# Inverse root of the variance for ten tiles: Newton's steps on GpSimd, where ScalarE took the root and VectorE the reciprocal

## What is computed

```python
def layer_norm(x, g, b):
    mu = jnp.mean(xf, axis=-1, keepdims=True)
    var = jnp.mean(jnp.square(xf - mu), axis=-1, keepdims=True)
    return (xf - mu) * lax.rsqrt(var + LN_EPS) * g + b
...
# in trunk_layer: 16 experts, each token goes to two of them
x = layer_norm(ALPHA * x + m, ln1_g, ln1_b)
x = layer_norm(ALPHA * x + hier_moe(x, w_router_group, w_router_expert, moe_w1, moe_w3, moe_w2),
               ln2_g, ln2_b)
```

## Time and profile before

| what | us |
|---|---|
| median of 3 runs | 1248.2 |
| lowest and highest of them | 1243.39, 1250.84 |
| the profiled execution | 1245.41 |
| its span, first to last instruction | 1243.7 |
| TensorE busy in the span | 1138.6 |
| VectorE busy | 788.6 |
| ScalarE busy | 536.3 |
| GpSimd busy | 183.1 |

### The profile page before, as it was taken

How to read it: one execution, slowest core, us unless ns; L and a number is a source line. 1 busy time by engine, 2 the same in 40 slices (tenths; PEclk the granted TensorE clock), 3 DMA queues, 4 the chain that set the end, 5 groups by cost and what they waited for, 6 DMA issues and landing times. The chain is left out here.

```text
span 1243.7 us, 20594 instructions
## 1 busy us (share of the span) xinstructions
PE 1138.6 (92%) x5700; PEld 1015.2 (82%) x5701; DVE 788.6 (63%) x1510; ACT 536.3 (43%) x686; POOL 183.1 (15%) x189
## 2 busy tenths in 40 slices
PE   6999999999999999999999974989998999899980
PEld 6999999999999999788888763768886777677760
DVE  4666454564465366566666467666754888778875
ACT  4464344444345346122222223445544756656530
POOL 1000000000000001003322224015001131222222
PEclk9999999999999999999999986899999999999995
DMA  5332598676946635425443316574766789877654
GB/s 182 123 102 65 129 159 117 75 155 85 118 87 223 243 100 180 144 83 175 151 137 135 89 69 243 201 290 171 264 249 251 273 277 339 299 286 272 218 204 152
DMA packets 86987, 221.06 MB, mean 178 GB/s; under 512 B 18992, under 2 KB 45648, under 8 KB 80656
## 3 DMA queue, kind: packets, MB, share of 16 engines
q1 hardware_dynamic: 57824, 129.90, 31.1%
q0 software_dynamic: 18160, 59.53, 14.3%
q10 hardware_dynamic: 10944, 30.95, 12.9%
HBM read 133.75 MB, written 86.58 MB: 177 GB/s over the span
## 5 line engine op out<-in xcount | busy, mean ns | idle before, releaser
L1391 PE MATMUL ps_h<-w_hi,xt_hi 128*128 (+1 forms) x328 | 135.2, 412 | 9.7 <-DVE w_lo L1048 6.2
L1391 PE MATMUL ps_h<-w_lo,xt_hi 128*128 (+1 forms) x328 | 131.0, 399 | 0.0
L1391 PE MATMUL ps_h<-w_hi,xt_lo 128*128 (+1 forms) x328 | 130.9, 399 | 0.0
L286 PE MATMUL ps_vb_c<-x_hi,w_hi 128*128 (+1 forms) x320 | 114.5, 358 | 10.9 <-DVE x_lo L460 10.9
L286 PE MATMUL ps_vb_c<-x_hi,w_lo 128*128 (+1 forms) x320 | 113.6, 355 | 0.0
L286 PE MATMUL ps_vb_c<-x_lo,w_hi 128*128 (+1 forms) x320 | 112.9, 353 | 0.0
L286 PE MATMUL ps_va_b<-x_hi,w_lo 128*128 (+1 forms) x320 | 112.7, 352 | 0.0
L286 PE MATMUL ps_va_b<-x_hi,w_hi 128*128 (+1 forms) x320 | 112.6, 352 | 0.0
L286 PE MATMUL ps_va_b<-x_lo,w_hi 128*128 (+1 forms) x320 | 111.8, 349 | 0.0
L1391 PEld LDWEIGHTS ps_h<-w_hi,xt_hi 128*128 128x128 f32 x328 | 63.5, 194 | 26.4 <-issue 13.9
L1048 DVE TENSOR_TENSOR w_lo<-w_raw,w_hi 128x2048 f32 (+1 forms) x32 | 73.1, 2287 | 6.8 <-ACT w_hi L1043 5.1
(11 more groups left out here) (337 smaller groups left out, 2622.4 us busy)
## 6 DMA issues: line engine op xcount, KB each, us to landing
w_raw<-in_w SPq DMA_DIRECT2D x48, 1024.0 KB
o_scr<-x_raw ACTq DMA_DIRECT2D x42, 512.0 KB, 8.0
w_lo_p<-xs_scr SPq DMA_DIRECT2D x41, 512.0 KB
o_scr<-w_lo_p SPq DMA_DIRECT2D x41, 512.0 KB
w_raw<-in_w_in POOLq DMA_DIRECT2D x19, 512.0 KB, 3.6
xs_scr<-x_raw ACTq DMA_DIRECT2D x17, 512.0 KB, 9.9
x_raw<-in_x_t SPq DMA_DIRECT2D x20, 416.0 KB, 3.4
x_hi_p<-y_scr SPq DMA_DIRECT2D x16, 512.0 KB, 4.3
```

The source lines that it names most:

```text
L286: mm = pe.matmul(ps[i][:, 0:CHUNK], w[:, i, k], x[:, k, bass.ds(c * CHUNK, CHUNK)], start=(k == 0 and n == 0), stop=(k == KT - 1 and n == 2))
L1391: mm = pe.matmul(ps_h[par][:], x[:, par, k], w[:, bass.ds(at, 1), k].rearrange("p o n -> p (o n)"), start=(k == 0 and n == 0), stop=(k == ...
```

## The change

For tiles 0 to 9 the root and the reciprocal are replaced. A new function `inverse_root` on GpSimd computes 1/sqrt(variance + constant) itself: it adds the constant, halves the bits of the number as an integer and subtracts them from a magic constant, which gives a first guess, and refines it by three of Newton's steps of two instructions each. With a last multiplication for the sign and the factors gathered on the way it is ten instructions on a column of 128 rows by one element. Each counts up the semaphore `s_nwt`, and the next waits for it. The chain waits for the aggregate (`s_mv`) and its last instruction counts up `s_rstd`, for which VectorE's second half of the normalisation waits, as before.

The chain is called in GpSimd's step ahead of `fetch` and `put`. ScalarE's `root` and its idle Silu, and VectorE's reciprocal, remain for tiles 10 to 16 (`known`).

```diff
+        def known(tile):
+
+            return isinstance(tile[0], int) and tile[0] >= FPAIR
...
+            def inverse_root(tile):
...
+                pool.wait_ge(s_mv, 1)
+                pool.wait_ge(s_mv, there)
+                at = [done]
+
+                def then(ins):
+                    ins.then_inc(s_nwt, 1)
+                    at[0] = count(pool, at[0] + 1)
+                    pool.wait_ge(s_nwt, 1)
+                    pool.wait_ge(s_nwt, at[0])
+
+                then(pool.tensor_scalar(t, mv[0:n, m, 1:2], LN_EPS, None, ALU.add))
+                then(pool.tensor_copy(bits, t.bitcast(I32)))
+                then(pool.tensor_scalar(guess, bits, -0.5, float(0x5f3759df), ALU.mult, ALU.add))
+                last = guess.bitcast(F32)
+                for i, (to, three) in enumerate(((y, 3.0), (nwt[0:n, 3:4], 12.0), (nwt[0:n, 4:5], 768.0))):
+                    then(pool.tensor_scalar(a, last, last, t, ALU.mult, ALU.mult))
+                    then(pool.tensor_scalar(to, a, -three, last, ALU.add, ALU.mult))
+                    last = to
+                pool.tensor_scalar(rstd[0:n, m:m + 1], last, -1.0 / 8192, None, ALU.mult).then_inc(s_rstd, 1)
...
                     stored = (h, h - 1) if par == 0 else (h, h)
+                    if add and not known(add):
+                        inverse_root(add)
 
                     if get:
                         fetch(get, stored)
...
-                if tiles and tiles[1]:
+                if tiles and tiles[1] and known(tiles[1]):
                     root(tiles[1])
...
-                dve.wait_ge(s_std, f + 1)
-                dve.reciprocal(rstd[0:n, m:m + 1], std[0:n, m:m + 1]).then_inc(s_rstd, 1)
+                if known(tile):
+                    dve.wait_ge(s_std, f + (1 - FPAIR))
+                    dve.reciprocal(rstd[0:n, m:m + 1], std[0:n, m:m + 1]).then_inc(s_rstd, 1)
```

More of the change, by code:

```diff
@@ L1114, in moe_phase @@
         std, rstd = sb("std2", [P, 2]), sb("rstd2", [P, 2])
+        nwt, nwt_i = sb("nwt", [P, 6]), sb("nwt_i", [P, 1], I32)
         eps, idle = sb("eps2", [P, 1]), sb("idle", [P, 1])
@@ L1133, in moe_phase @@
         s_v = [sem(f"s_v{i}") for i in range(5)]
+        s_nwt = sem("s_nwt")
         s_sum, s_bn, s_mv, s_std, s_rstd, s_fx, s_fn, s_y = (
@@ L1310, in fetch @@
                     pool.indirect_dma_start(to, None, o_scr[0:STEPS * P], bass.IndirectOffsetOnAxis(at, 0)).then_inc(s_v[b], 16)
+            def inverse_root(tile):
+                f, m = tile[0], tile[2] % 2
+                n = TAIL if early(f, 1) else P
+                t, y, a = nwt[0:n, 0:1], nwt[0:n, 1:2], nwt[0:n, 2:3]
+                bits, guess = nwt[0:n, 5:6], nwt_i[0:n]
+                done = count(pool, f * 9)
+                there = count(pool, f + 1)
+                pool.wait_ge(s_mv, 1)
[15 more added lines that the diff above has]
+                pool.tensor_scalar(rstd[0:n, m:m + 1], last, -1.0 / 8192, None, ALU.mult).then_inc(s_rstd, 1)
             def put(tile):
```

## The result

The change makes the kernel slower: median 1288.1 us of 4 runs against 1247.0 us of 4 of the kernel before on the same chip, **ratio 1.035 [1.032, 1.038]**, 41 us. The prediction was 1265 with a range from 1246 to 1290: right side, right place, and less than half the size. The profiled execution took 1286.20 us (span 1284.5, mean granted clock 0.945, was 0.962), 40.8 more than that of before.

A forecast was written before the change was run, and what follows sets the result against it. TensorE and VectorE together were taken to bound the stretch. Split intervals 12.9, plus 7.0 before tile 10, minus 1 of gain, made +18.9 us on 1245.4, or 1264.3; 1265 was forecast, range 1246 to 1290.

The forecast's parts named there:

- The queue: In GpSimd's queue the chain stands ahead of the next tile's COPY and two gathers, so the next row sum waits.
- The chain: GpSimd's ten dependent instructions: 0.4 us each, 10.4 us in a step with a weight split, 4.1 without.
- Tiles 5, 6 and 8: Tiles without a split: loop of 17.3 to 18.8 us against intervals of 21.6 and 22.1, adding nothing.
- Before tile 10: Tile 10's sum, one step after tile 9's, starts 7.4 us late, 7.0 after 0.4 to spare; landing 6.5.
- the subtraction of 12.0 us: VectorE idles 2.9 us per pair; 2.0 counted as made good in each of six split intervals, taken off the loss.
- the loop (25.2): From sum to sum with a split: statistics 2.84, chain 10.4, fetch 3.9, landing 8.0 us, against an interval of 21.2.
- the landing: Time from the second gather's end to the next row sum in pairs with a split, taken as 8.0 us.
- rival B: The cover holds: landing 5.3 us, instruction 0.28, loop 21.3; only tile 9 is late; 1245 to 1253 us, 22%.
- the fetch: GpSimd's COPY of row numbers to the end of the second gather, behind the chain, taken as 3.9 us.
- C: ScalarE's relief sends splits and weight transfers out earlier; a third of 30 us comes through: 1238 us, 5%.
- D: From about 0.55 us per instruction the chain itself is late and VectorE waits on it directly: 1278 to 1295, 13%.
- A: The forecast itself: the gathers come late, 1255 to 1285 us, 60%.

The follow-up runs named there:

- wait_only: The kernel before, with GpSimd waiting for the tile's aggregate ahead of the fetch for tiles 0 to 9, computing nothing; ratio 1.003.
- chain_after_fetch: The changed kernel with GpSimd's chain moved behind the fetch; ratio 1.006 to the kernel before.
- half_weights: The changed kernel with half the bytes in each transfer of the next weights from the third expert on; ratio 1.023 to the kernel before.
- split_5_5: The changed kernel with the chain cut in two, five instructions ahead of the fetch and five behind it; ratio 1.008 to the kernel before.
- one_step: The changed kernel with one of Newton's steps instead of three, six chain instructions instead of ten; ratio 1.019 to the kernel before.
- four_more: The changed kernel with four copies of the guess's instruction added, 14 in the chain; ratio 1.040 to the kernel before.
- root_kept: The changed kernel with root and reciprocal kept for all tiles and the chain writing an unused column; ratio 1.035 to the kernel before.
- no_root: The kernel before without root, table loads and idle Silu for tiles 0 to 9, reciprocal of a constant, no chain; ratio 0.996.

## Why the prediction was right in place and wrong in size

**What held.** The queue was the mechanism: the fetch behind the chain, shown by wait_only against chain_after_fetch. The chain has 0.34 to 0.53 us from start to start (predicted 0.4), 10.0 us with a split, once 11.6 (10.4), and 4.4 without (4.1). It is held by L1048, L1048 and L1057 as drawn. Tiles 5, 6 and 8 add nothing. Before tile 10 VectorE waits 5.2 us and the interval grows by 5.3 (7.0 predicted, a landing of 4.4 us where 6.5 was taken). GpSimd's timeline of the changed kernel, tile 10's second gather:

```profile
1204.01 0.98 POOL L1316 DMA_INDIRECT x_raw<-o_scr,id_f  x1 [0.30 <-issue]
```

And VectorE's timeline, tile 10's sum:

```profile
1209.36 1.23 DVE L1611 TENSOR_TENSOR w_hi_p<-w_hi_p,x_raw 128x1024 f32<-128x1024 f32 x1 [5.19 <-DMA x_raw<-o_scr,id_f]
```

**The step that failed first is the subtraction of 12.0 us, "what VectorE can make good".** The sum had set the loop (25.2) against the interval (21.2). When a loop is the longer of the two it is the interval, and VectorE's gaps already lie inside the landing, beside which it waits. The idle time shows it. From tile 0 to 5 VectorE idles 106.1 - 91.7 = 14.4 us before, 1.1 of them for gathers; after, 140.4 - 91.3 = 49.1, of which 36.6 for gathers. The rest went from 13.3 to 12.5. So 0.8 us were made good in five pairs where 2.0 were taken for each. By the same sum without this step the forecast would have been 1277 instead of 1265.

**The second is the landing.** 8.0 us was read from two pairs (7.88 and 8.38 by their rows) in which the gathers went out with the next weights: the second gather ends at 1022.65 where the weights start at 1022.09, and at 1066.03 where they start at 1066.06. After, it ends 4.9 to 5.4 us behind the weights' start, and a landing takes 10.1 to 11.2. The prediction itself said, against rival B, that the chain moves the gathers behind these transfers, and then didn't price it. half_weights shows that half of the weights' bytes are worth 1.1 to 3.5 us of a landing, 2.2 in the mean. How the landing follows the gathers' place isn't settled: in single pairs it is 8.4 us with the gathers 1.3 us behind (split_5_5), 10.7 at 2.1 (one_step), 11.2 at 5.0, 8.9 at 7.1 (four_more).

**The third is the fetch**, 4.65 us for 3.9: the COPY is held by the first half of the normalisation (1.10 instead of 0.18), and the first gather, beside the second half, takes 1.48 instead of 0.95; the gap between them was taken as 1.53 and is 0.81. I had named the locks for the chain and not gone on to the instructions behind it.

In numbers, the six intervals with a split were to grow by 12.9 and grew by 41.8: 12.0 of the difference is the subtraction, 16.9 landing and fetch, most of it the landing (10.4 us in the mean of the six, where 8.0 was taken).

Against it go 4.4 us by which the pairs from tile 5 to 7 and from 8 to 9 became shorter. That isn't ScalarE's relief: the interval from tile 5 to 6 is 22.4 us in the changed kernel and 22.3 in root_kept, but 26.7 in no_root. It is work done in the wait. While VectorE waits 6.6 us for the gathers of tile 5, TensorE goes on with what it has, so less is left for it in the next interval. Busy times by stretch, columns as above, from tile 5's sum to tile 6's, in the kernel before and in the changed one:

```profile
1074.40:1100.00 25.60, 22.60 (x102) 18.36 (x101) 18.41 (x20) 13.72 (x15) 5.11 (x6) 0.93 0.67 260
1105.40:1127.80 22.40, 18.52 (x79) 15.63 (x80) 18.35 (x20) 10.40 (x10) 7.14 (x14) 0.85 0.50 184
```

TensorE has 79 instructions there instead of 102, 79 in root_kept, 85 in one_step (21.4 us) and 83 in half_weights (21.2), but 107 in no_root, where no sum waits. So a little of the last wait is paid back behind it, where the loop no longer bounds the pair. The prediction had these pairs at nothing.

**The rivals.** B is refuted, with landings never at 5.3 in these pairs. C's 10 us of relief were 4.5 in no_root, 9 at most by its interval, and nothing in the changed kernel against root_kept; and C needed B. D's condition, over 0.55 us per instruction, did not come, and VectorE waited for the result once, for 0.5 us; D's time was reached by A's mechanism.

A gather's descriptors took 2.88 us across L1057 in split_5_5, against 0.94. By the exception of the Trainium skill (SBUF — State Buffer, "Who interferes with whom"), that descriptors pass beside a tensor_tensor, they would not have: for these gathers the runs decide against it, as the row of before had. The same section of the Trainium skill has GpSimd's reads of SBUF held beside such an instruction, and the gathers take their row numbers from there (`id_f`). Which of the two is held, the reading or the writing of descriptors, these runs can't tell.

## What to carry to other kernels

Work moved to an engine that is idle costs what stands behind it in that engine's queue: look for the loop that goes through it, add up its whole length, and if that exceeds the interval take it as the new interval, with nothing off for gaps elsewhere. Price a transfer's landing at the place to which the change moves it, not at the place where the trace has it. And where an engine is held up by another's instructions, go on through all that now falls under them, the consumer's own first half included.

## What the runs showed of the hardware

- A small dependent instruction of GpSimd (128x1) takes 0.18 to 0.35 us where nothing holds it, with 0.13 to 0.19 us (once 0.31, in four_more) from the end of one to the start of the next through a semaphore. A cast takes 0.18 to 0.19; the longer ones take one or two of their factors from columns.
- VectorE's scalar_tensor_tensor on two operands in SBUF holds GpSimd up as its tensor_tensor does: a COPY of 0.19 us took 1.10, and the wait for a chain behind it was 2.01 to 2.05 us in eight pairs of ten.
- Issued some 5 us behind 3 MB of weights, with the DMA share near 1, two gathers of 0.5 MB land 10.1 to 11.2 us after the second's instruction ends, and after 6.8 to 9.2 when half of those 3 MB is left out.
- TensorE, idle for 32 us of the 140 (6 of 106 before), had a mean granted clock of 0.88 in this stretch, where it had 0.98. Its busy time over the run grew by 8 us at the same instructions. Which part of the 41 us that is can't be read from these runs; of the 32 us TensorE waits 30.6 for VectorE's hidden product, behind the sum.
